# Three product sums of the first fast unit ahead, GpSimd held there, a buffer per square in the first norm, and all seven low parts of an activation pair on VectorE

## The reference

```
h = rms(x) * norm_mix                       # first norm, of layer 0 it opens the kernel
(13 parts) = split(h @ w_in)                # then three attention branches and gates
x = x + (ga*ya + gb*yb + gc*yc) @ w_o
h2 = rms(x) * norm_ffn
gt, up = split(h2 @ w_ffn_in)               # 2 x 2816 columns
x = x + (silu(gt) * up) @ w_ffn_out
```

## Time and profile before

| | |
|---|---|
| median of 3 runs | 2117.38 us |
| profiled execution | 2117.41 us, span 2115.6 us |
| PE busy | 2073.4 us (98%), 14418 matmuls |
| DVE busy | 1536.2 us (73%) |
| ACT busy | 1161.2 us (55%) |
| POOL busy | 529.4 us (25%) |
| 16 DMA engines | 97 GB/s mean |

### The profile page before, as it was taken

The page is one execution under the profiler, slowest core; times in us unless marked ns, Lnnn a source line. Parts: engine busy times, 40 slices in busy tenths (PEclk is TensorE's granted clock), DMA queues, the critical chain, the costliest instruction groups (busy, mean ns, idle before and its releaser), DMA issues.

```text
span 2115.6 us, 40337 instructions
## 1 busy us (share of the span) xinstructions
PE 2073.4 (98%) x14418; PEld 1936.3 (92%) x14418; DVE 1536.2 (73%) x3307; ACT 1161.2 (55%) x2565; POOL 529.4 (25%) x415
## 2 busy tenths in 40 slices
PE   8999999999999999999999999999999999999999
PEld 7998868888998999999999987788889989999999
DVE  5467877646848989898645678766477599898984
ACT  4236776566434666566432467665663356566652
POOL 1120030200021554445211200203000234544450
PEclk9999999999999999999999999999999999999999
DMA  5224224233330232222322331341424312222232
GB/s 195 92 85 139 90 79 134 78 94 131 124 120 31 78 103 71 90 76 92 109 99 83 116 117 68 102 139 60 148 78 130 110 44 77 91 75 95 71 105 76
DMA packets 95605, 205.97 MB, mean 97 GB/s; under 512 B 21232, under 2 KB 50544, under 8 KB 95088
## 3 DMA queue, kind: packets, MB, share of 16 engines
q1 hardware_dynamic: 95408, 203.40, 29.5%
HBM read 179.41 MB, written 23.95 MB: 96 GB/s over the span
## 4 chain that ended last, share of the span: by engine, by line
PE 78%; DVE 11%; ACT 4%; DVEq 3%; issue 2%; POOL 1%; DMA 0%; SPq 0%; ACTq 0%
PE ps L1092 15%; PE ps L1018 9%; PE ps L1579 9%; PE ps L1581 9%; PE ps L1580 9%; PE ps L1038 7%; PE ps L1104 5%; DVE op_lo L2764 3%; PE ps L1269 2%; PE ps L1289 2%; PE ps L1165 2%; PE ps L1210 1%; DVEq L2239 1%; PE ps L1383 1%; DVEq L2845 1%
## 5 line engine op out<-in xcount | busy, mean ns | idle before, releaser
L2246 DVE TENSOR_TENSOR w_lo<-raw,w_hi 128x1024 fp32r<-128x1024 f32 (+4 forms) x128 | 146.0, 1141 | 168.3 <-ACT w_hi L1625 163.8
L1092 PE MATMUL ps<-h_hi,w_hi 128*128 128x320 f32 x768 | 246.0, 320 | 0.0
L1092 PE MATMUL ps<-h_hi,w_lo 128*128 128x320 f32 x768 | 237.3, 309 | 0.0
L1092 PE MATMUL ps<-h_lo,w_hi 128*128 128x320 f32 x768 | 237.2, 309 | 0.0
L1625 ACT ACTIVATE w_hi<-raw 128x1024 fp32r<-128x1024 f32 (+4 forms) x128 | 125.8, 983 | 197.2 <-PE ps L1018 115.1
L2199 POOL TENSOR_TENSOR rsq<-ssq,mhalf 128x12 f32<-128x12 f32 (+3 forms) x56 | 117.0, 2090 | 418.8 <-DVE ssq L2358 359.2
L1579 PE MATMUL ps<-th_hi,op_hi 128*128 128x320 f32 x640 | 202.2, 316 | 15.0 <-DVE part L2832 15.0
L2764 DVE TENSOR_TENSOR op_lo<-w_sums,op_hi 128x512 fp32r<-128x512 f32 (+1 forms) x256 | 186.8, 730 | 17.0 <-ACT op_hi L1625 2.6
L1581 PE MATMUL ps<-th_hi,op_lo 128*128 128x320 f32 x640 | 199.1, 311 | 0.0
L1580 PE MATMUL ps<-th_lo,op_hi 128*128 128x320 f32 x640 | 199.0, 311 | 0.0
L1625 ACT ACTIVATE op_hi<-w_sums 128x512 fp32r<-128x512 f32 (+1 forms) x256 | 147.6, 588 | 89.1 <-PE ps L1581 75.7
(11 more groups left out here) (415 smaller groups left out, 6211.2 us busy)
## 6 DMA issues: line engine op xcount, KB each, us to landing
raw<-in_weights SPq DMA_DIRECT2D x176, 512.0 KB, 3.5
raw<-in_weights SPq DMA_DIRECT2D x72, 384.0 KB, 3.0
gates<-gst SPq DMA_DIRECT2D x72, 160.0 KB, 1.8
g<-gates SPq DMA_DIRECT2D x12, 960.0 KB, 6.8
ktb<-in_cache_fox_kt SPq DMA_DIRECT2D x16, 384.0 KB, 4.7
vc<-in_cache_fox_v SPq DMA_DIRECT2D x16, 384.0 KB, 3.7
out_y_t<-x_sb SPq DMA_DIRECT2D x12, 320.0 KB, 2.2
raw<-in_weights SPq DMA_DIRECT2D x8, 416.0 KB, 3.1
```

Of the source, the lines that this page charges most:

```text
L1092: mm = pe.matmul(ps[:, 5, 0:HALF], w[:, kk * P:(kk + 1) * P], h_pair[x][:, kk, half * HALF:(half + 1) * HALF], start=kk == 0 and n == 0, s ...
L2246: return dve.tensor_tensor(low[:, 0:width], raw[raw_slot(c)][:, 0:width], high[:, 0:width].bitcast(F32), ALU.subtract)
```

## The change

- The first norm's squares go into `first_squares`, one buffer per block k (in the space of "act"), so that ACT waits for no sum. VectorE now sums part 0, GpSimd part 1. The table copies move from the head of VectorE's program to behind `mean_square(0, 0)` and `diagonal(0, 0)`. Unread products: 2 instead of 7, 4 instead of 8. `norm_sum(0, 1)` comes after step 2 of part 0, `norm_spread(0, 1)` after step 3; `mean_square(0, 1)` in front of `rest(0, 0, 7)`.
- VectorE adds products 1, 2 and 3 of unit 0 before its pass over it, and GpSimd's sums for unit 1 wait for operand_lo(0, 5), not (0, 3).
- The two low parts of a pair that GpSimd made are made by VectorE (`pair_low_too`), at position 4, before and after pair_low 4 and 5.

```diff
+        first_squares = home("first_squares", [P, KD, NTOK], F32, "act")
...
-                    if first and p:
+                    if first and not p:
                         pe.wait_ge(first_summed.sem, KD - 2)
...
-                    unread_products(7)
+                    unread_products(2)
                     norm_sum(0, 0)
-                    unread_products(8)
+                    unread_products(4)
                     norm_spread(0, 0)
...
-                        if (p, k) == (0, 0):
+                        if (p, k) == (0, 0 if L else 2):
                             norm_sum(0, 1)
-                        if (p, k) == (0, 2):
+                        if (p, k) == (0, 2 if L else 3):
                             norm_spread(0, 1)
...
                     if first:
                         act.wait_ge(x0_in[4 * p + k // 2].sem, 16)
+                        act.activation(first_squares[:, k, PARTS[p]], x_sb[:, k, PARTS[p]], ACT.Square, scale=D ** -0.5).then_inc(squared.sem, 1)
+                        return
...
                     for k in range(KD):
                         square(0, k, 0)
+                    first_part(0)
                     for k in range(4):
-                        square(0, k, 1)
-                    first_part(0)
-                    for k in range(4, KD):
                         square(0, k, 1)
                     for k in range(KD):
                         norm_hi(0, 0, k)
-                        if k in (1, 5, 7):
-                            first_part({1: 1, 5: 2, 7: 3}[k])
+                        if k < 4:
+                            square(0, 4 + k, 1)
+                        if k in (1, 3, 5):
+                            first_part((k + 1) // 2)
...
                 if L == 0:
-                    sum_squares(0, 0, [(k, 0) for k in range(1, KD - 1)])
                     root(0, 0, 0)
+                    for k in range(1, KD - 1):
+                        total = square_sum[:, PARTS[1]]
+                        pool.wait_ge(squared.sem, square_at(True, k, 1) + 1)
+                        pool.drain()
+                        pool.tensor_tensor(total, first_squares[:, 0, PARTS[1]] if k == 1 else total, first_squares[:, k, PARTS[1]], ALU.add).then_inc(square_summed.sem, 1)
                     root(0, 0, 1)
...
-                def pair_low(m, r, i, src):
-
-                    pool.wait_ge(pair_hi.sem, pair_hi.at(L, 7 * m + r))
-                    pool.tensor_tensor(a_lo[i][:, m % 3, :], src, a_hi[i][:, m % 3, :].bitcast(F32), ALU.subtract).then_inc(pair_lo_too.sem, 1)
-
...
-                    pool.wait_ge(lo_made.sem, lo_made.at(L, made_by(s - 1, 3)))
+                    pool.wait_ge(lo_made.sem, lo_made.at(L, made_by(s - 1, 3 if s > 1 else 5)))
...
-                    if m is not None:
-                        pair_low(m, 4, 3, pair_first(m))
-                        pair_low(m, 7, 5, ff_act[1][:, 0:HALF])
...
                 if L == 0:
+                    for k in range(1, KD - 1):
+                        sum_first(k)
                     mean_square(0, 0)
-                    sum_first(1)
+                    table_out(0)
+                    table_out(2)
                     diagonal(0, 0)
-                    sum_first(2)
+                    table_out(1)
+                    table_out(3)
+                    dve.tensor_copy(bvec[:, :, SEQ:NTOK], ps[:, 4, :].rearrange("p (h n) -> p h n", h=DH)).then_inc(tab_late.sem, 1)
+                    scaled(0, 0, 0)
                     first_low(0)
-                    for k in (3, 4, 5):
-                        sum_first(k)
-                    scaled(0, 0, 0)
-                    sum_first(6)
                     for k in range(KD):
                         if k + 1 < KD:
                             scaled(0, 0, k + 1)
                         rest(0, 0, k)
-                        if k in (1, 5, 7):
-                            first_low({1: 1, 5: 2, 7: 3}[k])
-                mean_square(0, 1)
-                diagonal(0, 1)
+                        if k in (1, 3, 5):
+                            first_low((k + 1) // 2)
+                        if k == 6:
+                            mean_square(0, 1)
+                    diagonal(0, 1)
+                else:
+                    mean_square(0, 1)
+                    diagonal(0, 1)
...
                 operand_lo(0, 5)
+                dve.wait_ge(first_out.sem, first_out.at(L, 1))
+                product_sum(0, 1, part[0][:, :], sg[:, 0, second])
+                dve.drain()
+                product_sum(0, 2, part[1][:, :], part[0][:, :])
+                dve.drain()
                 operand_lo(0, 6)
+                product_sum(0, 3, part[1][:, :], part[1][:, :])
...
+                def pair_low_too(m, r, i, src):
+
+                    dve.wait_ge(pair_hi.sem, pair_hi.at(L, 7 * m + r))
+                    dve.tensor_tensor(a_lo[i][:, m % 3, :], src, a_hi[i][:, m % 3, :].bitcast(F32), ALU.subtract).then_inc(pair_lo_too.sem, 1)
...
                         if m is not None and pos == 4:
+                            pair_low_too(m, 4, 3, pair_first(m))
                             pair_low(m, 4)
                             pair_low(m, 5)
+                            pair_low_too(m, 7, 5, ff_act[1][:, first])
```

More of the change, by code:

```diff
@@ L998, in norm_sum @@
                         pe.wait_ge(square_summed.sem, square_summed.at(L, 2 * (KD - 2) * q + summed_at(first, KD - 2, p) + 1))
+                    last_squares = first_squares[:, KD - 1, :] if first else squares[:, 1, :]
                     for n, t in enumerate(PART_TILES[p]):
-                        for k, rows in enumerate((square_sum[:, t * P:(t + 1) * P], squares[:, 1, t * P:(t + 1) * P])):
+                        for k, rows in enumerate((square_sum[:, t * P:(t + 1) * P], last_squares[:, t * P:(t + 1) * P])):
                             mm = pe.matmul(ps[:, norm_banks(q, L, p)[0], 2 * n:2 * n + 2], rows, cst("ones", 0, 2), start=k == 0, stop=k == 1)
@@ L1656, in square @@
                     if k >= 2:
[L1657 to L1660, removed]
+                        act.wait_ge(square_summed.sem, square_summed.at(layer, 2 * (KD - 2) * q + summed_at(first, max(1, k - 2), p) + 1))
                     act.activation(squares[:, k % 2, PARTS[p]], x_sb[:, k, PARTS[p]], ACT.Square, scale=D ** -0.5).then_inc(squared.sem, 1)
@@ L2200, in _ @@
                 norm_roots(1, L)
-                def pair_low(m, r, i, src):
-                    pool.wait_ge(pair_hi.sem, pair_hi.at(L, 7 * m + r))
-                    pool.tensor_tensor(a_lo[i][:, m % 3, :], src, a_hi[i][:, m % 3, :].bitcast(F32), ALU.subtract).then_inc(pair_lo_too.sem, 1)
                 for s in range(1, len(FAST)):
-                    c, width, m = fast_chunk(s), fast_width(s), paired(s - 1) if s else None
+                    c, width = fast_chunk(s), fast_width(s)
                     for u in range(2):
                         pool.wait_ge(chunk_landed[raw_slot(c + u)].sem, chunk_landed[raw_slot(c + u)].at(L, 16 * LANDED[c + u]))
-                    pool.wait_ge(lo_made.sem, lo_made.at(L, made_by(s - 1, 3)))
+                    pool.wait_ge(lo_made.sem, lo_made.at(L, made_by(s - 1, 3 if s > 1 else 5)))
                     if s == 1:
@@ L2230, in _ @@
         def _(dve):
[L2231 to L2234, removed]
             dve.wait_ge(norms_in.sem, 16)
@@ L2319, in sum_first, with table_out @@
                 def sum_first(k):
-                    a = square_sum[:, PARTS[1]]
-                    dve.wait_ge(squared.sem, square_at(True, k, 1) + 1)
+                    a = square_sum[:, PARTS[0]]
+                    dve.wait_ge(squared.sem, square_at(True, k, 0) + 1)
                     dve.drain()
-                    dve.tensor_tensor(a, squares[:, 0, PARTS[1]] if k == 1 else a, squares[:, k % 2, PARTS[1]], ALU.add).then_inc(first_summed.sem, 1)
+                    dve.tensor_tensor(a, first_squares[:, 0, PARTS[0]] if k == 1 else a, first_squares[:, k, PARTS[0]], ALU.add).then_inc(first_summed.sem, 1)
+                def table_out(h):
+                    dve.wait_ge(tab_done.sem, DH)
+                    dve.tensor_copy(bvec[:, h, 0:SEQ], ps[:, h, :])
                 if L == 0:
+                    for k in range(1, KD - 1):
+                        sum_first(k)
                     mean_square(0, 0)
-                    sum_first(1)
+                    table_out(0)
+                    table_out(2)
                     diagonal(0, 0)
-                    sum_first(2)
+                    table_out(1)
+                    table_out(3)
+                    dve.tensor_copy(bvec[:, :, SEQ:NTOK], ps[:, 4, :].rearrange("p (h n) -> p h n", h=DH)).then_inc(tab_late.sem, 1)
+                    scaled(0, 0, 0)
                     first_low(0)
-                    for k in (3, 4, 5):
-                        sum_first(k)
-                    scaled(0, 0, 0)
-                    sum_first(6)
                     for k in range(KD):
```

(12 more changed lines are left out.)

2 lines of the change are left out of this document (1 added, 1 removed).

## The result

The kernel after takes 2133.26 us (median of 4, 2131.52 to 2134.23), the kernel before 2117.01 beside it (2114.78 to 2120.63): ratio 1.0076 [1.0063, 1.0089], 16 us slower. The forecast was 2127.1 and its range ended at 2131.5: the sign was right, the size was not. The profiled execution took 2133.61 us (span 2131.7) against 2117.41 (2115.6).

What follows compares the result with a forecast made beforehand. TensorE holds 78% of the wait chain, but VectorE, taking turns with GpSimd, sets the waits around unit 1. 2117.4 + 8.5 (4.25 per layer, two layers) + 1.2 (first norm) = 2127.1 us; range 2112.5 to 2131.5.

Steps and rivals of the forecast that it cites:

- Sums ahead and pair 0, unit 0: Units 0 and 1: stall at product 5 goes, TensorE waits some 7 us before product 3 of unit 1; +0.8 us per layer.
- part 2: Pair 0: GpSimd's first three sums for unit 2 take turns with pair_total 0, pair_total 1, pair_low 0; 3 x 1.1 us.
- It is hidden, since VectorE is late for unit 2 as well: Unit 1: the slow clock after the 7 us wait before product 3 costs nothing.
- rival D: Unit 1: the slow clock after the 7 us outlasts VectorE's lead; 2 x 1.7 us more, 2131 us; chance 0.10.
- First norm: Opening: first projection earlier, but TensorE idle 2.9 us before part 1, then slow clock; +1.2 us, bounds -1.5 and +2.5.
- Last pairs: Units 4, 14, 24: pair_low 5 comes late for product 1 of the next unit; +0.9 us each, 2.7 per layer.
- Middle pairs: Units 2, 10, 12, 20, 22: VectorE's low parts and GpSimd's sums take turns; +0.15 us each, 0.75 per layer.
- Rival B: Pairs: VectorE is relieved if weight sums fall on instructions reading PSUM; -5 us, with the norm 2114; chance 0.12.

Runs made afterwards that it cites:

- e4: Kernel after with 28 products nobody reads before product 3 of unit 1 in both layers; 2128.81 us, ratio 1.0057 against the kernel before.
- e12: Kernel after, with GpSimd's sums held until operand_lo 5 only after the last pairs (units 4, 14, 24); 2126.88 us, ratio 1.0041 against the kernel before.
- e2: Kernel before with unit 0's three sums ahead and GpSimd held there, low parts still on GpSimd; 2117.03 us, ratio 1.0006.
- e10: As e8, but without the three sums of unit 0 ahead; 2109.05 us, ratio 0.9957 against the kernel before.
- e11: As e8, with 24 products nobody reads before product 3 of unit 1; 2108.26 us, ratio 0.9957 against the kernel before.
- e6: Kernel after with the hold: in every pair pass GpSimd's sums for unit s + 2 wait for operand_lo(s + 1, 5), not 3; 2113.56 us, 0.9979 against before.
- e8: Kernel after with the hold of e6 and the norm order of e5; 2110.28 us, ratio 0.9965 against the kernel before.
- e5: Kernel before with the change's first norm, but TensorE's old order and mean_square(0, 1) after rest 5; 2117.88 us, ratio 0.9996 against the kernel before.
- e7: Kernel before with the pairs' low parts on VectorE and the hold of e6, no sums ahead, old first norm; 2113.26 us, ratio 0.9974.
- e3: Kernel before with only the two low parts of each pair moved to VectorE; 2126.16 us, ratio 1.0046.

## Why the prediction was wrong in its size

- **Sums ahead and pair 0, unit 0: right.** No wait at product 5, 7 us at product 3 of unit 1, sum 6 late, +0.8 and +1.4 us against +0.8. VectorE after, in units 0 and 1, and GpSimd beside it:

```profile
682.28 3.60 DVE L2773 TENSOR_TENSOR op_lo<-w_sums,op_hi 128x512 fp32r<-128x512 f32 x3 [0.86 <-ACT op_hi L1627]
...
686.55 1.42 DVE L2820 TENSOR_TENSOR ff_act<-ff_act,ff_act 128x320 f32<-128x320 f32 x1
687.89 1.58 DVE L2827 TENSOR_TENSOR a_lo<-ff_act,a_hi 128x320 fp32r<-128x320 f32 x1
689.57 1.38 DVE L2820 TENSOR_TENSOR ff_act<-ff_act,sg 128x320 f32<-128x320 f32 x1
...
696.04 0.48 DVE L2766 TENSOR_TENSOR part<-part,ps 128x320 f32<-128x320 f32 x1
```

```profile
686.05 1.57 POOL L2214 TENSOR_TENSOR w_sums<-raw 128x512 f32<-128x512 f32 x1 [1.32 <-DVE op_lo L2773]
...
689.28 1.31 POOL L2218 TENSOR_TENSOR w_sums<-raw,raw 128x512 f32<-128x512 f32 x1 [0.16 <-issue]
```

  The two pair_totals and the low part took 1.42, 1.58 and 1.38 us, about 1.0 more each, as worked out in part 2; sum 6 starts at 696.04, which less the opening's 4.2 is 691.8, where 692.0 stood.

- **"It is hidden, since VectorE is late for unit 2 as well": the failed step.** The prediction put the slow clock behind the 7 us at nothing. In the kernel after it comes through with 1.6 us a layer, rival D's mechanism, and e4 gives 1.4 and 1.8 of it back by keeping TensorE occupied. The step was reasoned from the earlier trace rows, where VectorE sets the path up to 710.95. But that chain ran past a stall of 4 us which lay before VectorE's sum; the new one ends with it, and from 696.57 on some twenty matmuls of TensorE, 0.27 us apart instead of 0.147, stand on the path: 2.5 us lost, 1.6 of it for good. VectorE is late for unit 2, but only by enough to take up 0.9 of them. The 1.6 is the number of this trace and no constant: the same stretch cost 0.9 and 0.3 us in e12 with the same stall, 0.3 and 1.7 in e2. With the hold, where VectorE has more to catch up in unit 1 (TensorE's wait of 1.5 us there in e10 and e11), the step came true in both layers of e6 and in layer 0 of e8: the offset grows by 0.8 us over the stretch with the slow clock (e6, e8) as without it (e10, e11).

- **First norm: the mis-sized term, 4.2 us against 1.2.** Its events came in the order written (first projection at 21.23, spread behind k = 3, part 1 after 2.94 us of idle at a clock of 0.53). Two sizes were off. The spread came at 34.97 and not at 32.6 at the latest: 0.5 us because the first projection began at 21.23 and not 20.7, 1.0 because 16 matmuls behind its idle were 0.32 us apart where before nine were (7 x 0.147), and 0.7 because the last five matmuls of step k = 3 were slow as well, behind the wait of 0.68 us at 32.16. The idle of 2.94 and the slow clock behind it (ten matmuls, 1.5 us) then cost what was worked out. So part 1 starts 3.3 us late (39.39 against 36.10), loses 1.5 more, and 0.6 of the 4.8 are absorbed before the fast units. e5 shows that the order causes it: without the idle in front of part 1 nothing is lost in the median.

- **Last pairs: right.** +0.7 to +1.0 us against +0.9, three a layer. GpSimd's sums and VectorE's low parts of unit 14 alternate as the prediction has them (alone, one low part takes 0.48 us and two take 0.88):

```profile
858.44 0.84 DVE L2832 TENSOR_TENSOR a_lo<-sg,a_hi 128x320 fp32r<-128x320 f32 x1
859.21 2.52 DVE L2827 TENSOR_TENSOR a_lo<-ff_act,a_hi 128x320 fp32r<-128x320 f32 x2
```

- **Middle pairs: right**, +0.2 to +0.3 us each against +0.15.

- **Rival B** named the right relief under the wrong condition. The weight sums did not fall on instructions that read PSUM; they fell on the low parts. Only once the hold placed them elsewhere (e6, e7) did VectorE's low parts pay. The sentence drawn from the Trainium skill, page "GPSIMD Engine Reference" (Engine selection), that elementwise work belongs on VectorE, gave 0.46% slower without the hold (e3) and 0.26% faster with it (e7): here the measurement decides, and it says that the move pays or not by where GpSimd's next sums fall.

- **The range** took D as an alternative to the forecast. It was an addition to it, and with the norm at its upper bound of 2.5 the same bounds would have given 2127.1 + 1.3 + 3.4 = 2131.8; the norm's own bound was 1.7 us too low as well. With the two measured terms in place of the written ones the sum closes: 2117.4 + 8.5 + 2 x 1.6 + 4.2 = 2133.3, against 2133.6. That it closes so well is partly luck: the 1.6 contains unit 2's pair, which the 8.5 has too, the other terms together are 0.9 us higher in the trace than written, and the 0.45 us that fall away between the layers are in no term.

## What to carry to other kernels

- Where two engines take turns at the operands, freeing one of work lets its next work start sooner, on top of whatever the other does then. Place that work, by the wait that releases it, before judging the move.
- A stall of TensorE that is taken away at one product is worth only what the engine feeding it gains until the next wait.
- Where stalls are merged into a longer one, give the slow clock behind it a term of its own. Here it cost between nothing and 1.7 us a layer, by how many matmuls were slow and by how far the feeding engine was behind; neither could be read off the kernel before.
- In this kernel a norm's sum two steps later and its spread one step later left TensorE with nothing to do in front of part 1, and cost about 4 us: before an order is changed, look what covers the wait behind it.

## What the runs showed of the hardware that was not expected

- The slow clock's cost after an idle is not one number, and the idle's length does not set it. After 2.9 us of idle, nine matmuls were slow in the kernel before and 16 in the kernel after, at the same place. In e7 an idle of 3.9 us before product 5 of unit 0 was followed by 12 matmuls at the slow clock (0.27 us apart) in layer 0 and by 21 in layer 1. After 7.07 us the 1.2 GHz level was held through the whole of 697 to 702 in the kernel after, and e12 had 19 and 14 such matmuls behind the same wait.
- The clock column of the windows view can print 1.00 where nothing was recorded. In this window of the kernel after the matmuls of the first projection start 0.32 us apart up to 26.5, against 0.17 from 26.8 on:

```profile
21.00:24.00 3.00, 2.77 (x9) 2.80 (x10) 2.85 (x7) 1.72 (x5) 1.56 (x1) 1.00 0.24 101
```

  The trace's first entry of the clock is at 26.75 us, and the view prints 1.00 for 1 to 4 us too, where TensorE hasn't done anything yet. The spacing is that of 23 to 26 us of the kernel before, granted 0.51. In an opening, read the spacing of the matmuls and not this column.
- With the same opening code, part 1 began at 36.10 (before), 39.94 (e2), 35.16 (e3) and 35.89 us (e7), and with the squares of the change in the old order at 33.66 (e5) and 38.18 us (e8). Single traces differ there by up to 4.8 us, so effects of the opening were read from medians and those of the fast units from the start of unit 0 on. What makes it vary stays open.
